# One of three weight streams moved from SyncE's DMA queue to ScalarE's

## The reference

```python
for e in range(N_EXPERTS):                      # 32 experts
    hdn = jax.nn.silu(xf @ w1[e]) * (xf @ w3[e])   # w1, w3: 1024 x 512
    acc = acc + combine[:, e:e + 1] * (hdn @ w2[e])  # w2: 512 x 1024
...
x = _layer_norm(DEEPNORM_ALPHA * x + f, ln2_g, ln2_b)
```

## Time and profile before

| what | value |
|---|---|
| median of 3 runs | 693.96 us (691.85 to 695.86) |
| the profiled execution's own time | 698.17 us |
| its span | 696.4 us |
| granted TensorE clock, mean | 0.982 |
| busy: PE, PEld, DVE, ACT, POOL | 598.3, 413.3, 307.1, 217.7, 160.0 us |
| q1 (SP), q0 (POOL), q10 (ACT): MB moved | 220.92, 11.78, 2.67 |

### The profile page before, as it was taken

One profiled execution on the slowest core, in us unless ns is written; L12 is line 12 of the kernel. 1 busy time (PEld: TensorE's weight loads), 2 busy tenths in 40 slices (PEclk: granted clock), 3 DMA queues, 4 the chain that ended last, 5 costly groups with the idle time before them and its releaser, 6 DMA issues.

```text
span 696.4 us, 10578 instructions
## 1 busy us (share of the span) xinstructions
PE 598.3 (86%) x4194; PEld 413.3 (59%) x4194; DVE 307.1 (44%) x785; ACT 217.7 (31%) x316; POOL 160.0 (23%) x187
## 2 busy tenths in 40 slices
PE   5999999999999999999999777777788677768783
PEld 5999999977886555555555344444444444445351
DVE  3454286615567415354535243333333433333544
ACT  3242313401122314534453242414323232424040
POOL 1000000000000323344243323332222232233333
PEclk8899999999999999999999999999999999999998
DMA  9990330746199999999999999999999999999991
GB/s 248 259 336 18 135 121 1 300 186 271 61 360 423 329 415 417 416 417 419 421 417 414 416 417 420 421 420 422 421 420 420 419 419 418 421 418 418 420 405 64
DMA packets 45786, 236.07 MB, mean 339 GB/s; under 512 B 13700, under 2 KB 18308, under 8 KB 28888
## 3 DMA queue, kind: packets, MB, share of 16 engines
q1 hardware_dynamic: 32191, 220.92, 78.8%
q0 software_dynamic: 12688, 11.78, 5.1%
q10 hardware_dynamic: 857, 2.67, 1.0%
HBM read 238.22 MB, written 30.20 MB: 385 GB/s over the span
## 4 chain that ended last, share of the span: by engine, by line
PE 43%; DMA 33%; SPq 16%; DVE 5%; issue 1%; ACT 1%; POOL 0%; POOLq 0%; DVEq 0%; ACTq 0%
DMA blocks<-in_w 24%; PE ps L548 14%; PE ps L723 11%; SPq L401 10%; PE ps L605 7%; DMA eleventh_block<-in_w 7%; PE ps L744 6%; SPq L405 4%; DMA blocks<-in_w_in 1%; PE ps L634 1%; PE ps L709 1%; PE ps L732 1%; PE ps L618 1%; SPq L425 1%; DVE blocks L1283 1%
## 5 line engine op out<-in xcount | busy, mean ns | idle before, releaser
L723 PE MATMUL ps<-blocks,ln 128*64 128x256 f32 x1952 | 224.8, 383 | 45.6 <-DMA blocks<-in_w 44.1
L723 PEld LDWEIGHTS ps<-blocks,ln 128*64 128x64 f32 x1952 | 151.6, 138 | 120.2 <-issue 67.9
L744 PE MATMUL ps<-blocks,hT 128*64 128x512 f32 x480 | 111.0, 604 | 22.1 <-DMA blocks<-in_w 21.3
L744 PEld LDWEIGHTS ps<-blocks,hT 128*64 128x64 f32 x480 | 32.8, 138 | 82.0 <-issue 52.8
L1018 ACT ACTIVATE std<-rstd,eps 128x1 f32<-128x1 f32 x32 | 9.4, 294 | 211.6 <-DVEq L1570 211.5
L1538 DVE SCALAR_TENSOR_TENSOR h_rows<-silu,slot_gate,ps 128x256 f32<-128x256 f32 x33 | 15.8, 480 | 97.2 <-PE ps L723 97.0
L1126 POOL DMA_INDIRECT out<-prev,final_row x32 | 32.1, 1002 | 86.8 <-DVE prev L1576 85.9
L1122 POOL DMA_INDIRECT prev<-first_outputs,final_row x32 | 34.0, 1062 | 77.6 <-DMA first_outputs<-ye,first_row 46.7
L548 PE MATMUL ps<-xT_high,w_in_high 128*128 128x288 f32 x256 | 42.3, 309 | 4.7 <-ACT w_in_high L827 3.5
L968 ACT ACT_TABLE_LOAD x30 | 38.5, 1283 | 20.8 <-PE ps L723 20.4
L1549 DVE TENSOR_TENSOR ye<-ye,ps 128x512 f32<-128x512 f32 x16 | 11.0, 688 | 71.8 <-PE ps L744 71.8
(11 more groups left out here) (242 smaller groups left out, 765.6 us busy)
## 6 DMA issues: line engine op xcount, KB each, us to landing
blocks<-in_w SPq DMA_DIRECT2D x86, 2048.0 KB, 43.2
eleventh_block<-in_w SPq DMA_DIRECT2D x8, 2048.0 KB, 44.8
blocks<-in_w_in SPq DMA_DIRECT2D x3, 2048.0 KB, 10.0
blocks<-in_w_out SPq DMA_DIRECT2D x2, 2048.0 KB, 7.8
blocks<-in_w SPq DMA_DIRECT2D x4, 1024.0 KB, 37.6
x_tok<-in_x_prompt SPq DMA_DIRECT2D x4, 512.0 KB, 5.4
blocks<-in_w_in SPq DMA_DIRECT2D x4, 512.0 KB, 11.9
first_outputs<-in_x_prompt SPq DMA_DIRECT2D x4, 512.0 KB, 8.3
```

The costliest lines, as they stand in the source:

```text
L723: mm = pe.matmul(ps[64 * g:64 * g + 64, bank, 0:FH], x, w[:, k, g * FH:(g + 1) * FH], start=(k == 0), stop=(k == KD - 1))
L744: mm = pe.matmul(ps[64 * g:64 * g + 64, BY, :], hT[:, k % 2, k // 2 * SLOTS:(k // 2 + 1) * SLOTS], w[:, k, g * DH:(g + 1) * DH], start=(k ...
```

## The change

ACT gets its own copy of `block_free` and `expert_of` (both become functions of the issuing engine) and a `load_w3`. In the loop over tiles it issues w3 of tile t + 3 right after the SiLU of tile t, for t from 3 to 26. Of w3 of tiles 6 to 29 there are 23 loads, since tile 9 has none. SP leaves them out of its loop and issues all others as before. Blocks, semaphores and their values stay the same. ACT waits once for `order_ready` ahead of the loop.

```diff
+BY_ACT = {("w3", t) for t in range(EARLY + 1, STAGGERED)}
...
+        def block_free(eng, n):
+
+            if n == EARLY_BLOCKS:
+                eng.wait_ge(fetched, 1)
+                eng.wait_ge(x1_stored, 16 * NT)
+                return
+            kind, t = LOADS[n - EARLY_BLOCKS - 1]
+            eng.wait_ge({"w1": h1_done, "w3": h_done, "w2": y_done}[kind], t + 2 if t == SHARED else t + 1)
...
             for n in range(ORDERED, len(LOADS)):
-                block_free(n)
-                load(n)
+                if LOADS[n] not in BY_ACT:
+                    block_free(sp, n)
+                    load(n)
...
+            expert_of = chooser(act)
+
+            def load_w3(t):
+
+                n = PLACE["w3", t]
+                block_free(act, n)
+                src = w3[bass.DynSlice(expert_of(t), 1)].rearrange("e d f -> (e d) f")
+                act.dma_start(in_block(HOME[n]), src.rearrange("(p c) f -> p c f", c=KD)).then_inc(block_loaded[HOME[n]], 16)
...
+            act.wait_ge(order_ready, 1)
             for t in range(2, E):
                 silu_of(t)
+                if t > 2 and ("w3", t + 3) in BY_ACT and ("w3", t + 3) in PLACE:
+                    load_w3(t + 3)
```

More of the change, by code:

```diff
@@ L352, in wait, with chooser, expert_of @@
                 eng.wait_ge(semaphore, value)
+        def block_free(eng, n):
[5 more added lines that the diff above has]
+            eng.wait_ge({"w1": h1_done, "w3": h_done, "w2": y_done}[kind], t + 2 if t == SHARED else t + 1)
+        def chooser(eng):
+            chosen = {}
+            def expert_of(t):
+                p = t if t <= SHARED else t - 1
+                if p < EARLY:
+                    return p
+                if t not in chosen:
+                    chosen[t] = eng.value_load(order[0:1, p:p + 1], min_val=0, max_val=E - 1)
+                return chosen[t]
+            return expert_of
         turn_banks = [4, 5, 0, 1, 2, 3, 4, 5, 2, 3]
@@ L406, in load_out @@
                              src.rearrange("(g p c) d -> p g c d", g=2, c=KF // 2)).then_inc(block_loaded[b], 16)
[L408 to L426, removed]
+            expert_of = chooser(sp)
             def load(n):
```

## The result

| | before | after |
|---|---|---|
| median of 4 runs each | 692.9 us (691.43 to 695.86) | 718.6 us (717.0 to 720.52) |
| the profiled execution, its span | 698.17, 696.4 us | 720.52, 718.5 us |
| granted TensorE clock, mean | 0.982 | 0.928 |
| DMA share, GB/s, 440 to 600 us | 1.01, 420 | 1.00, 410 |

The ratio is 1.0355 (95% interval 1.0328 to 1.0383). Against the 693.96 us from which the forecast set out the kernel is 24.6 us slower. The forecast was 709 us, 15 us slower; the measured time lies inside the range of 692 to 722.

A forecast was written before the change was run, and what follows sets the result against it. The expert stage was taken as bound by the weight stream at full DMA rate. PE 24 us late at tile 14, less 8 of end slack and 1 recovered, gives 15 us on 693.96: 709 us, range 692 to 722.

The forecast's parts named there:

- What bounds the kernel before: Expert stage: weights stream at full DMA rate, share 1.01 at 420 GB/s, 16.0 us per tile from tile 14 on.
- ACT's work costs nothing: ACT behind the SiLU: 23 loads of 1.0 us each are covered by its waits; without cover 23 us.
- A turn per filled queue, and rounds of twice the bytes: DMA engines: one packet per filled queue in turn; w3 beside q1 cuts rounds per tile from 35 to 26, POOL needing 24.4.
- 24.4 turns then take 11.55 x 24.4 / 19.3 = 14.6 us: Tiles before 14: POOL's turns lengthen a tile by 3.0 us, over 8 tiles making PE 24 us late at tile 14.
- check by latency: From add_y over store_first and load_prev to prev: 33 us, 10 us of wait in the first phase, about none later.
- After tile 14 both kernels go at 16.0 us per tile: From tile 14 on bytes set the pace and 94% of turns suffice for POOL; PE stays 24 us late.
- rival (c): POOL's dependent DMAs set the pace to the end, 13 us on top, 722 us, DMA share below 0.97; chance 0.14 with worse.
- The end: From w1 of tile 29 to PE's end: 57 us of work in 65.4, slack 8 us, plus 1 us recovered in tiles 27 to 29.
- Overtaking: w3 lands ahead of w1 and w2 by up to three blocks, 16 us of lateness, inside the other and not added.
- (a): No change, 694 us: the stream hides it all, PE under 9 us late at tile 29; chance 0.22.
- (b): Faster, 684 to 690 us: two filled queues close gaps between packets; chance 0.04.
- (d): ACT's issue blocks like SP's, 4.7 us instead of 0.34: 27 us late at most, inside the range; no separate chance.

The follow-up runs named there:

- 1: Kernel after the change, but ACT's DMA brings only 1 KB to a scratch tensor and SP issues w3 as before; 694.76 us, ratio 1.0002.
- 8: Kernel after the change, with only w3 of the even tiles 6 to 28 on ACT's queue (12 loads instead of 23); 693.93 us, ratio 1.0014.
- 9: Kernel after the change, with store_first and load_prev moving 64 of their 128 rows; 693.79 us, ratio 1.0008.
- 11: Kernel after the change, with ACT's loads only for w3 of tiles 18 to 29 (12 loads); 693.95 us, ratio 0.9997.
- 2: Kernel before the change, with w1 and w3 of tiles 6 to 31 loaded as two 1 MB transfers, halving packets to 8 KB; 698.56 us, ratio 1.0082.
- 3: Kernel after the change, with w1 and w3 of tiles 6 to 31 as two 1 MB transfers on both queues, halving packets; 697.35 us, ratio 1.0058.
- 4: Kernel before the change, nothing on ACT's queue, w2 loaded in runs of 16 KB instead of two of 8 KB per partition; 705.12 us, ratio 1.0179.
- Kernel 7: Kernel after the change, with w2 of tiles 5 to 28 on ACT's queue instead of w3, which SP issues; 721.2 us, ratio 1.0382.
- kernel 5: Kernel after the change, without send_sample, so the sample rows are not written; 707.32 us, ratio 1.019.
- Kernel 6: Kernel after the change, with 24 extra identity matmuls in odd tiles 7 to 29 ahead of w2's product; 720.03 us, ratio 1.0339.
- kernel 12: Kernel after the change, with each w3 as four 512 KB DMAs on ACT's queue; 719.81 us, ratio 1.0371.
- kernel 10: Kernel after the change, with ACT's loads only for w3 of tiles 6 to 23 (17 of 23); median 702.35 us, ratio 1.014.

## Why the prediction was right, and where it was off

**What bounds the kernel before: right.** Where the stream keeps its rate and PE is in time for it again by its end, the time does not move (1, 8, 9, 11), and the split, which lowers the rate from 420 to 416 GB/s, costs 0.8% (2).

**ACT's work costs nothing: right** (1: 1.0002). Its issues took 0.34 to 0.35 us. SP's fell from 4.7 us to 0.34 us (median of 17 between 329 and 612 us), and nobody gained by it, as said. Its reason is another matter: SP now waits for PE to free a block ahead of most issues, 196 us in 19 waits at w2 alone from 300 to 690 us, so its queue is no longer filled far ahead.

**A turn per filled queue, and rounds of twice the bytes: right in kind.** 3 removes the loss by halving the packets, 4 makes it by lengthening them with no third queue. The packets came as forecast (4014, 1420, 3833 against 4160, 1440, 3900), and the landings of `store_first` in the chain from 300 us on, 12.5 to 17.7 us, and of `load_prev`, 14.4, lie in the 12 to 18 that were named. Kernel 7 shows the limit of "each packet of SP lets one of POOL through": POOL's 3608 packets had 2878 of SP's.

**"24.4 turns then take 11.55 x 24.4 / 19.3 = 14.6 us": this step failed.** It took the pace from the total of POOL's turns in a tile, as if its transfers filled every turn. They don't: `load_prev` waits for a landing, and q0 used 85% of q1's turns. What sets the pace is the serial loop: 16.1 us from one `store_first` to the next between 338.76 and 403.36 (four intervals), and 16.65 us per PE tile from 8 to 14. PE came to tile 14 30 us late, not 24. Kernels 5 and 9 show that it is the loop and not the sum. The prediction had the loop in hand, as its check by latency: 1 + 13.5 + 1 + 17.7 = 33 us for two tiles, against the measured 32.2 (338.76 to 370.94) and 32.4 (370.94 to 403.36). It used it only to see that the slack was gone, and read `store_first` and `load_prev` of one tile in a row, not that a store stands in q0 behind the `load_prev` ahead of it. That the two sums agree is luck in part: its sum holds one landing of each kind, the loop two landings of `store_first`. Two tiles in 32 to 33 us are 16 to 16.5 each, not 14.6. The sum at tile 14 came near because a second step was off the other way: PE falls behind from tile 8, not from tile 6 (2 us late at tile 9, 16 at tile 10). Six tiles at 16.65 - 11.7 = 4.9 us are the 30 us; the prediction had eight at 3.0. Eight at 4.9 would have been 40 us.

**"After tile 14 both kernels go at 16.0 us per tile": the number right, the reason wrong.** From tile 14 to 29 PE took 242.2 us in 15 tiles, 16.1 each, as before (242.0). It was the loop that held it at that, with no wait for a block left. That is rival (c)'s mechanism, the chain that sets the pace to the end, but without its sign (the DMA share stayed at 1.01 until 500 us and at 0.98 to 1.01 until 620) and without its further loss of 13 us. Why loop and stream have the same pace is not shown. It may be chance, or the one may adjust to the other: PE frees the blocks that the stream fills, and the stream ran dry for a moment at 580 us. Where the loop is a little shorter, PE wins the lateness back: 22 us to -1 in kernel 8, 24 to 4 in kernel 9, 26 to 17 in kernel 5.

**The end: slack right, recovery 0 instead of 1.** From w1 of tile 29 to PE's end it took 708.75 - 651.46 = 57.3 us where 57 was worked out, so 8.1 of 30.2 us are absorbed and 22.1 stay. The sum should have stood at 30 - 8 - 0 = 22 us, which is what the profiled executions show (720.52 - 698.17 = 22.35). So of the 9.6 us by which the forecast was short, 6 belong to the two steps up to tile 14, 1 to the recovery, 2.3 to the profiled executions, of which the one before lay 4.2 us above its median and the one after 1.9, and the rest is rounding. Two more signs missed: the share fell below 1 for the last 38 us (0.17 from 680 to 690 us), not 20, and the slowing began two tiles later.

**Overtaking: right.** 9 to 17 us in kernel 11 (16 forecast), and given back.

**Not foreseen: the clock.** The mean granted clock fell from 0.982 to 0.928 and a matmul of w2 took 690 ns in the mean instead of 604. Kernel 6, with its 5 us of extra work at the end taken off, leaves a few us for it at most.

**The rivals.** (a), no change, wanted PE under 9 us late at tile 29, since POOL's landings would stay within their slack. Kernel 8, with 12 loads, meets the first (-1 us) without the second (22 waits for `prev`); 23 loads meet neither. (b) found nothing: two slices ran at 427 GB/s where 423 was the most before, but from 440 to 600 us the rate was 410 instead of 420. (d) came only with kernel 12's small requests. The Trainium skill's "DMA: Bandwidth & Descriptors", section "Issuing engines are not separate DMA queues", would have given 694 us here and in kernel 7, and that kernels 1 and after be alike. They are 1.0002 and 1.0355. Its statement that all queues share the same 16 engines agrees with the traces (a share of 1.01 before and 1.00 after, from 440 to 600 us, with the bytes divided among the queues); that only issue time is at stake does not.

**Open**: the spread of kernel 10, how much the clock cost, why the loop's pace is the stream's, and whether the loss goes if `store_first` is issued ahead of `load_prev`, which was not tried.

## What to carry to other kernels

A second queue of large packets did not add bandwidth to a stream that was already at its rate; it lengthened every round in which a queue of small, dependent transfers got its turn. Look for the serial loop of such transfers (landing, issue, landing), count what stands in the queue inside the loop, and hold its time per step against the stream's: the total of turns says too little. Then follow the lateness to the end, where a slack that one can read off the timeline is taken off it once.

## What the runs showed of the hardware that was not expected

- A longer run in one queue is enough to slow another queue: w2 in runs of 16 KB instead of 8 KB (q1 4330 packets instead of 5604 in 160 us, at 421 GB/s instead of 420) cost 1.8%, with the landings of `store_first` at 10.4 us instead of 7.9. Those of `load_prev` were at 8.9 instead of 10.0: what stands ahead of a transfer in its own queue counts too, and the two were not separated. The other way, halved packets brought `load_prev` from 10.0 to 7.7 us for 0.8% of the time.
- The issue of a transfer can hold ACT, as it holds SP (4.7 us before): 12.2 us at most with four transfers per matrix, 0.35 us with one. I take it that the queue is full then; how many it takes wasn't measured.
- PE's granted clock followed its waits: 0.84 from 340 to 380 us, where PE was held by DVE, and 1.00 from 640 to 700 us, where it hardly waited; with extra matmuls in between the mean rose from 0.928 to 0.978.
